# A differential, latent and stick-breaking attention trunk: another order of the latent projections, of the weight splits and of the second mixer's sums

## The chip, the cores and the metric

The kernel runs on one core of a Trainium2 chip. The metric is the device time of one execution in microseconds, a median of several runs. The engines are TensorE (PE; its weight loads are PEld in the profile), VectorE (DVE), ScalarE (ACT), GpSimd (POOL) and SyncE (SP, which here issues nearly all DMAs). Each engine runs its own list of instructions in order; they meet at semaphores.

## The reference

Two layers on one sequence of 512 frames, width 1024. Layer 0 runs two mixers on one input projection, differential attention (4 heads) and multi-head latent attention (8 heads); layer 1 runs stick-breaking attention (16 heads). Each layer ends with a SwiGLU network of inner width 2816.

```python
def diff_mla_mixer(h, pos, ...):
    a_q, a_k, a_v, b_ql, b_kvl, b_kr = split_cols(h @ w_in, AB_IN_SPLITS)  # 512,512,512,256,128,32
    ...
    q_b = (rms_norm(b_ql, b_q_a_norm) @ b_w_q_b).reshape(B, S, B_HEADS, B_NOPE_DIM + B_ROPE_DIM)
    kv_b = (rms_norm(b_kvl, b_kv_a_norm) @ b_w_kv_b).reshape(B, S, B_HEADS, B_NOPE_DIM + B_V_DIM)
    ...
    out_b = latent_attention(q_nope, q_rope, k_nope, k_rope, b_v, (B_NOPE_DIM + B_ROPE_DIM) ** -0.5)
    mixed = jnp.concatenate([out_a..., out_b...], axis=-1)
    return mixed @ w_out

def stick_breaking_attention(q, k, v, scale):      # for one block of queries lo..hi
    z = jnp.einsum('bqhd,bkhd->bhqk', q[:, lo:hi], k[:, :hi]) * scale
    sp = jnp.where(mask, jax.nn.softplus(z), 0.0)
    tail = lax.cumsum(sp, axis=3, reverse=True) - sp
    w = jnp.where(mask, jnp.exp(jax.nn.log_sigmoid(z) - tail), 0.0)
    return jnp.einsum('bhqk,bkhd->bqhd', w, v[:, :hi])

def reference(x, ...):
    for l in range(DEPTH):                          # DEPTH = 2
        h = rms_norm(x, norm_mix[l])
        x = x + (diff_mla_mixer(h, ...) if l % 2 == 0 else stick_breaking_mixer(h, ...))
        x = x + swiglu(rms_norm(x, norm_ffn[l]), ...)
    return x
```

## The kernel before, in words

**Products.** Activations lie transposed (features on partitions, 512 frames along the free axis). Each float32 product is made of three products in the fp32r format: both operands are split into a high and a low part, and high times high, high times low and low times high are summed in PSUM.

**Weights.** They come in numbered chunks `g` of 128 partitions by up to 1408 columns into three slots (`WSLOTS`) in turn. For a chunk SP issues the load into `wraw` (`load_chunk`, L312) once the low part of the chunk three earlier is made; ACT copies it into `w_hi` (`split_hi`, L319) once PE has finished the chunk three earlier; POOL subtracts, `w_lo = wraw - w_hi` (`split_lo`, L331). Where in ACT's list a split stands is written by hand (`hi_static(act, g)`); POOL takes the chunks in their order, between its other work.

**Order.** Every engine's list is written out by hand in its own block at the end of the program; the small functions (`bq_pe`, `bq_act`, `bq_dve` and so on) are called there in the order in which they run, and no planner moves them.

**Token stage.** Here the weights are the moving operand and a 128x128 tile of the activations is the stationary one, so that frames come out on the partitions. PE makes the latent projection (`lat_pe`, chunks 0 to 3), the first differential queries (`pj_pe` for p = 0, chunks 4 and 5), and then for each half `hf` of the eight latent heads four query tiles (`bq_pe`, six matmuls of 384 columns) and four key and value tiles (`bkv_pe`, three matmuls of 512 columns), chunks 6 to 9. ACT evacuates and squares a tile, DVE sums the squares (`bq_dve`; `bkv_dve` also copies the keys and makes the low part of the values). A query tile waits for the square of the tile two earlier, a key tile for DVE's low part of the tile three earlier. When all eight tiles of a half are summed, DVE makes the means (`b_mean_dve`), ACT the inverse roots (`rs_act`), POOL a Newton step (`rs_newton_pool`) and then the rotation and scaling of two heads (`b_pair_pool`, L921 to L931). Chunk 10 is split by ACT right behind `rs_act` of half 0, chunk 11 two query tiles later. `rope_kr_dve` rotates the keys that all heads share. The squares of the differential queries go through one buffer, `pj_sq`: ACT writes the second half (`qk_act`, L973) after DVE has summed the first (`qk_dve`, L995).

**Second mixer.** Eight pairs of heads. In a pair PE makes the scores of both heads (`c_scores_pe`), then projects the next pair's queries, sums the first head's tails (`c_tail_pe`, L1490), projects the keys, sums the second head's tails, multiplies with the values (`c_values_pe`, L1521) and projects the next values. Between scores and tails lie three blocks of |z|, exp and log on ACT (`c_chain_act`) and of softplus and its split on DVE (`c_chain_dve`; L1479 makes the low part, from two operands in SBUF). A tail waits for all three blocks and goes through the key blocks in order. Before the first pair's chain ACT splits three chunks in a row. In the last pair PE fills its time with products of the output projection that are already possible (`out_early_pe`, L368): output chunk 0 up to tile 5, then chunk 1, tile 6 of chunk 0, chunk 2.

**Output projection.** `out_act` waits for a finished row of x, norms it, and then splits the chunk three ahead. The three chunks of `OUT_EARLY` need only their last tile then; chunk 3 is the first that runs whole.

## Time and profile before

| | us |
|---|---|
| median of 3 runs | 1286.64 (1285.88 to 1288.28) |
| the profiled execution | 1289.69 |
| its span | 1287.9 |
| PE busy (weight loads) | 1258.3 (1071.2) |
| DVE, ACT, POOL busy | 570.0, 584.7, 528.9 |

The profile is of one execution; its durations are those of that execution, which took 3.05 us more than the median. PE's matmuls overlap, so that the distance between two starts, and not a row's own duration, tells what one costs. A row of the timeline ends with the idle time before it in brackets and with what ended it. POOL's durations are rough. PEclk is the granted clock of TensorE as a mean over a stretch, 1.00 being 2.4 GHz.

### The profile page before, as it was taken

The numbers are of one execution on the slowest core, as the hardware profiler recorded it, in microseconds if no ns is written. First come the engines' busy times: TensorE is split into PE (matmuls) and PEld (weight loads), VectorE is DVE, ScalarE is ACT, GpSimd is POOL, SyncE is SP. The second block draws the span as 40 slices with busy tenths as digits, with TensorE's granted clock in tenths as the row PEclk, the third lists the DMA queues.
The fourth block names the chain that finished last, engine by engine and source line by source line (L and its number), as shares of the span: only waits on it lengthen the run. The fifth ranks groups of instructions, "written<-read, shape, count | busy, mean of one in ns | idle before, by whom it ended". The sixth has DMA issues, their size and how long they took to land.

```text
span 1287.9 us, 16944 instructions
## 1 busy us (share of the span) xinstructions
PE 1258.3 (98%) x6308; PEld 1071.2 (83%) x6308; DVE 570.0 (44%) x995; ACT 584.7 (45%) x959; POOL 528.9 (41%) x267
## 2 busy tenths in 40 slices
PE   8899989999999999999999999998999999999999
PEld 7799978888888888888878888887888888888887
DVE  7756677653221112221278888886322210122210
ACT  5657865554322122233367777885433321222310
POOL 4465520265445344445432222221744444344442
PEclk9999999999999999999999999999999999999999
DMA  5221110033233222332211111110322242222331
GB/s 203 84 69 46 38 50 17 17 111 115 98 114 101 80 82 98 98 129 84 82 54 56 54 49 65 56 59 16 115 88 95 101 135 72 86 96 96 113 125 41
DMA packets 29143, 105.84 MB, mean 82 GB/s; under 512 B 3360, under 2 KB 3616, under 8 KB 29088
## 3 DMA queue, kind: packets, MB, share of 16 engines
q1 hardware_dynamic: 28944, 105.07, 24.5%
q8 instruction: 37, 0.61, 0.2%
q14 instruction: 18, 0.15, 0.0%
q10 hardware_dynamic: 144, 0.02, 0.0%
HBM read 102.98 MB, written 2.10 MB: 82 GB/s over the span
## 4 chain that ended last, share of the span: by engine, by line
PE 89%; DVE 7%; ACT 2%; issue 1%; POOL 1%; DMA 0%; ACTq 0%; POOLq 0%; DVEq 0%
PE bank L342 23%; PE bank L343 22%; PE bank L346 22%; PE bank L1490 4%; PE bank L1521 2%; PE bank L1117 1%; PE bank L1451 1%; PE bank L958 1%; PE bank L960 1%; PE bank L962 1%; PE bank L1066 1%; PE bank L1356 1%; PE bank L1046 1%; PE bank L1357 1%; PE bank L1358 1%
## 5 line engine op out<-in xcount | busy, mean ns | idle before, releaser
L331 POOL TENSOR_TENSOR w_lo<-wraw,w_hi 128x1024 fp32r<-128x1024 f32 (+4 forms) x180 | 456.4, 2537 | 696.7 <-ACT w_hi L319 696.7
L342 PE MATMUL bank<-h_hi,w_hi 128*128 128x512 f32 x896 | 350.8, 391 | 0.0
L343 PE MATMUL bank<-h_lo,w_hi 128*128 128x512 f32 x896 | 349.0, 389 | 0.0
L319 ACT ACTIVATE w_hi<-wraw 128x1024 fp32r<-128x1024 f32 (+4 forms) x180 | 197.9, 1101 | 236.5 <-DVE x L664 125.6
L346 PE MATMUL bank<-h_hi,w_lo 128*128 128x512 f32 x896 | 221.8, 389 | 0.0
L342 PEld LDWEIGHTS bank<-h_hi,w_hi 128*128 128x128 f32 x896 | 168.3, 188 | 35.7 <-issue 1.1
L346 PEld LDWEIGHTS bank<-h_hi,w_lo 128*128 128x128 f32 x896 | 168.2, 188 | 34.9
L343 PEld LDWEIGHTS bank<-h_lo,w_hi 128*128 128x128 f32 x896 | 168.3, 188 | 34.2
L342 PE MATMUL bank<-f_hi,w_hi 128*128 128x512 f32 x352 | 136.9, 389 | 0.0
L343 PE MATMUL bank<-f_lo,w_hi 128*128 128x512 f32 x352 | 136.9, 389 | 0.0
L627 ACT ACTIVATE f_hi<-fa 128x512 f32 (+1 forms) x44 | 27.9, 633 | 217.1 <-DVE fa L653 217.1
L650 DVE TENSOR_TENSOR fu<-bank,rstd 128x512 f32<-128x512 f32 x44 | 30.4, 691 | 194.8 <-PE bank L346 194.8
L664 DVE TENSOR_TENSOR x<-bank,x 128x512 f32<-128x512 f32 x32 | 22.1, 692 | 197.9 <-PE bank L346 197.9
L346 PE MATMUL bank<-f_hi,w_lo 128*128 128x512 f32 x352 | 85.6, 389 | 0.0
L342 PEld LDWEIGHTS bank<-f_hi,w_hi 128*128 128x128 f32 x352 | 66.1, 188 | 13.7
L346 PEld LDWEIGHTS bank<-f_hi,w_lo 128*128 128x128 f32 x352 | 66.1, 188 | 13.7
L343 PEld LDWEIGHTS bank<-f_lo,w_hi 128*128 128x128 f32 x352 | 66.1, 188 | 13.7
L648 DVE TENSOR_TENSOR fy<-bank,rstd 128x512 f32<-128x512 f32 x44 | 30.4, 692 | 101.0 <-PE bank L346 100.5
L958 PE MATMUL bank<-w_hi,h_hi 128*128 128x256 f32 x192 | 55.8, 291 | 0.0
L447 ACT ACTIVATE h_hi<-x,vec 128x512 fp32r<-128x512 f32 x32 | 23.0, 719 | 69.1 <-DVE x L664 40.2
L960 PE MATMUL bank<-w_hi,h_lo 128*128 128x256 f32 x192 | 54.3, 283 | 0.0
L962 PE MATMUL bank<-w_lo,h_hi 128*128 128x256 f32 x192 | 54.3, 283 | 0.0
(277 smaller groups left out, 2007.0 us busy)
## 6 DMA issues: line engine op xcount, KB each, us to landing
wraw<-in_w_in SPq DMA_DIRECT2D x120, 512.0 KB, 3.2
wraw<-in_w_down SPq DMA_DIRECT2D x32, 704.0 KB, 4.1
wraw<-in_w_ab SPq DMA_DIRECT2D x20, 512.0 KB, 3.3
x<-in_xt SPq DMA_DIRECT2D x8, 256.0 KB, 5.9
out<-x SPq DMA_DIRECT2D x8, 256.0 KB, 2.0
wraw<-in_w_ab SPq DMA_DIRECT2D x4, 416.0 KB, 5.9
wraw<-in_w_ab SPq DMA_DIRECT2D x2, 384.0 KB, 3.0
wraw<-in_w_ab SPq DMA_DIRECT2D x2, 256.0 KB, 2.8
```

The lines of the kernel that those rows point to most:

```text
L319: nc.scalar.activation(whi[:, s, 0:width], wraw[:, s, 0:width], ACT.Copy).then_inc(S("w_hi"), 1)
L331: nc.gpsimd.tensor_tensor(wlo[:, s, 0:width], wraw[:, s, 0:width], whi[:, s, 0:width], ALU.subtract).then_inc(S("w_lo"), 1)
L342: nc.tensor.matmul(out_bank, w, src_hi[kt], start=(kt == 0), stop=False)
L343: nc.tensor.matmul(out_bank, w, src_lo[kt], start=False, stop=False)
L346: return nc.tensor.matmul(out_bank, wlo[:, s, kt * P:(kt + 1) * P], src_hi[kt], start=False, stop=(kt == n - 1))
L627: nc.scalar.activation(tile_at(f_of[L][0], f), as3(fa[:], f), ACT.Copy).then_inc(S("net_hi"), 1)
L648: nc.vector.tensor_tensor(fy[:], bank[2 * j][:], rstd[:], ALU.mult).then_inc(S("net_y"), 1)
L650: nc.vector.tensor_tensor(fu[:], bank[2 * j + 1][:], rstd[:], ALU.mult).then_inc(S("net_u"), 1)
L958: nc.tensor.matmul(o, tok(hhi, 4 * c + k, i), whi[:, slot(g), w], start=(c == 0 and k == 0 and i % 2 == 0), stop=False, skip_group_check=True)
L960: nc.tensor.matmul(o, tok(hlo, 4 * c + k, i), whi[:, slot(g), w], start=False, stop=False, skip_group_check=True)
L962: last = nc.tensor.matmul(o, tok(hhi, 4 * c + k, i), wlo[:, slot(g), w], start=False, stop=(c == 1 and k == 3), skip_group_check=True)
L1490: last = nc.tensor.matmul(z, cmats[:, 0 if src == kb else 1, :], t[j][:, TO[src]:TO[src] + w], start=False, stop=True, skip_group_check=True)
```

## The change

Four parts:

1. **Latent queries and keys alternate** (`B_ORDER`) on PE, ACT and DVE; the last key column block (`lat_lo_dve(dve, 2)`) comes before `rope_kr_dve`, which goes behind the second query tile; `kr_trans_pe` and `kr_hi_act` go behind the half.
2. **Two square buffers**: `pj_sq` gets two halves, and the square of tile n waits for the sum of n - 2.
3. **Token-stage weights start 48 elements (192 bytes) into their slot** (`token_at`), for all chunks before `G_OB` = 20, in the load, in both splits and in the matmuls.
4. **Second mixer.** The first pair's first tail and the last pair's second tail go by source block: block `src` needs only DVE's part `src + 1`. The splits of the second and third chunk move from before the first pair's chain to behind its fourth and sixth block. Tile 6 of output chunk 0 moves from behind the last values to ahead of the last tail. `out_act` splits chunks 3 to 7 before it waits for the row of x.

```diff
+def token_at(g):
+    return 48 if g < G_OB else 0
...
-    def load_chunk(sp, g, s, src, width):
+    def load_chunk(sp, g, s, src, width, at=0):
         wait(sp, "w_lo", g - (WSLOTS - 1))
-        sp.dma_start(wraw[:, s, 0:width], src).then_inc(S(f"w_in{s}"), 16)
+        sp.dma_start(wraw[:, s, at:at + width], src).then_inc(S(f"w_in{s}"), 16)
...
     def out_act(act, g0, L, n):
         for d in range(KT):
+            if d < 5:
+                hi_static(act, g0 + d + 3)
             act.wait_ge(S("out_x"), L * KT + d + 1)
             norm_act(act, n, d)
-            hi_static(act, g0 + d + 3)
+            if d >= 5:
+                hi_static(act, g0 + d + 3)
...
+    B_ORDER = ((0, 0), (0, 1), (1, 0), (0, 2), (1, 1), (0, 3), (1, 2), (1, 3))
...
-            c = slice(k * BQ_N, (k + 1) * BQ_N)
+            c = slice(token_at(g) + k * BQ_N, token_at(g) + (k + 1) * BQ_N)
...
-        wait(act, "pj_sum", n)
-        nc.scalar.activation(pj_sq[:], bank[PJ[t]][:], ACT.Square).then_inc(S("pj_sq"), 1)
+        wait(act, "pj_sum", n - 1)
+        nc.scalar.activation(pj_sq[:, t, :], bank[PJ[t]][:], ACT.Square).then_inc(S("pj_sq"), 1)
...
     def c_tail_pe(pe, u, j):
+        if isinstance(u, int) and (u, j) in ((0, 0), (C_PAIRS - 1, 1)):
+            for src in range(NB):
+                if src < 3:
+                    pe.wait_ge(S(f"c_slo{j}"), u * 3 + (src + 1))
+                w = TW[src]
+                for kb in range(src + 1):
+                    b, o = ZAT[kb]
+                    z = bank[ZB[j][b]][:, o + TW[kb] - w:o + TW[kb]]
+                    for t in (cshi, cslo):
+                        last = nc.tensor.matmul(z, cmats[:, 0 if src == kb else 1, :], t[j][:, TO[src]:TO[src] + w],
+                                                start=False, stop=True, skip_group_check=True)
+                    if src == NB - 1 and kb != 2:
+                        last.then_inc(S(f"c_tail{j}"), 1)
+            return
         pe.wait_ge(S(f"c_slo{j}"), u * 3 + 3)
...
-            for i in range(NB):
-                bq_act(act, 0, i)
-            hi_static(act, 9)
-            for i in range(NB):
-                bkv_act(act, 0, i)
+            for what, i in B_ORDER:
+                (bq_act, bkv_act)[what](act, 0, i)
+                if (what, i) == (0, 3):
+                    hi_static(act, 9)
             kr_hi_act(act)
...
-            rope_kr_dve(dve)
             lat_lo_dve(dve, 2)
...
+            for what, i in B_ORDER:
+                (bq_dve, bkv_dve)[what](dve, 0, i)
+                if (what, i) == (0, 1):
+                    rope_kr_dve(dve)
...
                     c_chain_act(act, u, 1, 0)
+                    if late is not None:
+                        late(1)
                     c_chain_act(act, u, 1, 1)
                     c_chain_act(act, u, 1, 2)
+                    if late is not None:
+                        act.wait_ge(S("c_vy"), 1)
+                        late(2)
...
-            c_act(0, 1, lambda c: hi_static(act, G_C + 6 + c))
+            c_act(0, 1, lambda c: hi_static(act, G_C + 6 + c), lambda c: hi_static(act, G_C + 3 + c))
...
                     c_vt_pe(pe, u)
+                    if nxt is None:
+                        pe.wait_ge(S("c_mlo"), C_HEADS - 2)
+                        out_early_pe(pe, G_OUT1, 1, 0, (KT - 2,))
```

Three places show how the lists move. ACT in the token stage, before: the two squares of the first differential queries (`pj_sq`), the split of chunk 8 (`w_hi<-wraw` of 768 columns), then the query tiles (`qb` and `bq_sq`).

```order
L973 ACTIVATE pj_sq_83<-bank6 128x512
L973 ACTIVATE pj_sq_83<-bank7 128x512
L319 ACTIVATE w_hi_51<-wraw_50 128x768
L861 ACTIVATE qb_63<-bank0 128x4x96
L864 ACTIVATE bq_sq_84<-bank0 128x384
L861 ACTIVATE qb_63<-bank1 128x4x96
L864 ACTIVATE bq_sq_84<-bank1 128x384
L861 ACTIVATE qb_63<-bank0 128x4x96
L864 ACTIVATE bq_sq_84<-bank0 128x384
```

ACT at the same place now:

```order
L981 ACTIVATE pj_sq_83<-bank6 128x512
L981 ACTIVATE pj_sq_83<-bank7 128x512
L323 ACTIVATE w_hi_51<-wraw_50 128x768
L869 ACTIVATE qb_63<-bank0 128x4x96
L872 ACTIVATE bq_sq_84<-bank0 128x384
L869 ACTIVATE qb_63<-bank1 128x4x96
L872 ACTIVATE bq_sq_84<-bank1 128x384
L884 ACTIVATE vb_hi_65<-bank2 128x256
L887 ACTIVATE bk_sq_82<-bank2 128x256
L869 ACTIVATE qb_63<-bank0 128x4x96
L872 ACTIVATE bq_sq_84<-bank0 128x384
```

The key and value tiles (`vb_hi`, `bk_sq`) come in between; the rows ahead of them stand as before.

ACT at the second mixer's start, before: `cq_hi` and `ck` are the first pair's operands, `ca0` and `ca1` the chains of its two heads, three rows a block.

```order
L1543 ACTIVATE ck_119<-cyk_122 64x512 x2
L319 ACTIVATE w_hi_51<-wraw_50 128x1024 x3
L1463 ACTIVATE ca0_130<-bank0 128x512
L1465 ACTIVATE ca0_130<-ca0_130 128x512
L1467 ACTIVATE ca0_130<-ca0_130 128x512
L1463 ACTIVATE ca0_130<-bank1 128x384
```

The same place now, up to the sixth block of the chain:

```order
L1565 ACTIVATE ck_119<-cyk_122 64x512 x2
L323 ACTIVATE w_hi_51<-wraw_50 128x1024
L1471 ACTIVATE ca0_130<-bank0 128x512
L1473 ACTIVATE ca0_130<-ca0_130 128x512
```

and behind the fourth block (`ca1` from bank3):

```order
L1475 ACTIVATE ca1_131<-ca1_131 128x512
L323 ACTIVATE w_hi_51<-wraw_50 128x1024
L1471 ACTIVATE ca1_131<-bank4 128x384
L1473 ACTIVATE ca1_131<-ca1_131 128x384
L1475 ACTIVATE ca1_131<-ca1_131 128x384
L1471 ACTIVATE ca1_131<-bank5 128x512
L1473 ACTIVATE ca1_131<-ca1_131 128x512
L1475 ACTIVATE ca1_131<-ca1_131 128x512
L323 ACTIVATE w_hi_51<-wraw_50 128x1024
L1568 ACTIVATE cq_hi_117<-cyq_121 64x512 x4
```

One split is left ahead of the chain, the second stands behind its fourth block and the third behind its sixth.

PE in the last pair, before, from the transposes of the values (`cyv`) on; `cs1` is the second head's operand, `mixed` belongs to the output projection.

```order
L1566 MATMUL bank7<-mat_53,cyv_123 128x128 x4
L1490 MATMUL bank3<-cs1_hi_128,cmats_124 128x512
L1490 MATMUL bank3<-cs1_lo_129,cmats_124 128x512
L1490 MATMUL bank3<-cs1_hi_128,cmats_124 128x384
L1490 MATMUL bank3<-cs1_lo_129,cmats_124 128x384
L1490 MATMUL bank3<-cs1_hi_128,cmats_124 128x256
L1490 MATMUL bank3<-cs1_lo_129,cmats_124 128x256
L1490 MATMUL bank3<-cs1_hi_128,cmats_124 128x256
L1490 MATMUL bank3<-cs1_lo_129,cmats_124 128x256
```

The same place now:

```order
L1588 MATMUL bank7<-mat_53,cyv_123 128x128 x4
L372 MATMUL bank6<-mixed_hi_61,w_hi_51 128x512
L372 MATMUL bank6<-mixed_lo_62,w_hi_51 128x512
L372 MATMUL bank6<-mixed_hi_61,w_lo_52 128x512
L1500 MATMUL bank3<-cs1_hi_128,cmats_124 128x512
L1500 MATMUL bank3<-cs1_lo_129,cmats_124 128x512
L1500 MATMUL bank3<-cs1_hi_128,cmats_124 128x384
L1500 MATMUL bank3<-cs1_lo_129,cmats_124 128x384
L1500 MATMUL bank4<-cs1_hi_128,cmats_124 128x384
L1500 MATMUL bank4<-cs1_lo_129,cmats_124 128x384
L1500 MATMUL bank3<-cs1_hi_128,cmats_124 128x256
```

Three products of the output projection come first, and the sums take block 0 (512 columns), block 1 (384) and then block 2 (256) across the banks instead of bank after bank.

## Rows read from the trace of the kernel before

**Rows 1.** Stretches: us, busy time (instructions) of each engine, PEclk (granted clock), DMA share, GB/s
```profile
43.80:47.50 3.70, 0.14 (x1) 0.00 (x0) 2.98 (x7) 2.13 (x5) 0.73 (x1) 1.00 0.30 117
47.50:55.00 7.50, 7.32 (x29) 6.21 (x30) 4.39 (x15) 5.08 (x13) 3.95 (x3) 0.77 0.28 81
280.00:640.00 360.00, 360.00 (x1598) 298.42 (x1597) 81.13 (x117) 110.44 (x129) 171.27 (x71) 1.00 0.30 98
660.00:680.00 20.00, 17.83 (x91) 15.57 (x90) 19.52 (x28) 13.12 (x24) 4.36 (x2) 0.91 0.24 79
860.00:895.00 35.00, 31.21 (x162) 26.56 (x160) 24.22 (x42) 19.30 (x34) 2.41 (x1) 0.95 0.09 31
```

**Rows 2.** Timeline, PE, token stage: start, us, engine line op out<-in, form, [idle before <-releaser]
```profile
47.51 0.45 PE L836 MATMUL bank<-w_hi,ql_hi 128*128 128x384 f32 x1 [3.58 <-ACT bq_sq L864]
...
70.93 0.39 PE L958 MATMUL bank<-w_hi,h_hi 128*128 128x256 f32 x1
```

**Rows 3.** Timeline, ACT, token stage
```profile
45.37 0.60 ACT L973 ACTIVATE pj_sq<-bank 128x512 f32<-128x512 f32 x1 [4.00 <-DVE tiny L995]
...
58.40 1.05 ACT L319 ACTIVATE w_hi<-wraw 128x1024 fp32r<-128x1024 f32 x1
```

**Rows 4.** Timeline, DVE, token stage
```profile
40.65 0.27 DVE L790 MEMSET krpad<- 128x256 f32 x1
...
42.67 0.74 DVE L780 SCALAR_TENSOR_TENSOR kvl_lo<-bank,vec,kvl_hi 128x512 fp32r<-128x512 f32 x1
...
47.86 0.41 DVE L869 TENSOR_REDUCE tiny<-bq_sq 128x4 f32<-128x256 f32 x1
...
48.38 0.41 DVE L869 TENSOR_REDUCE tiny<-bq_sq 128x4 f32<-128x256 f32 x1
...
54.32 0.41 DVE L886 COPY kb<-bank 128x256 f32<-128x256 f32 x1
...
55.31 0.41 DVE L886 COPY kb<-bank 128x256 f32<-128x256 f32 x1
```

**Rows 5.** Timeline, POOL, token stage
```profile
59.53 2.41 POOL L331 TENSOR_TENSOR w_lo<-wraw,w_hi 128x1024 fp32r<-128x1024 f32 x1 [3.72 <-ACT w_hi L319]
...
68.49 2.39 POOL L331 TENSOR_TENSOR w_lo<-wraw,w_hi 128x1024 fp32r<-128x1024 f32 x1
```

**Rows 6.** Timeline, PE, second mixer, first pair and start of the second
```profile
665.81 0.50 PE L1490 MATMUL bank<-cs_hi,cmats 128*128 128x512 f32 x1 [2.17 <-DVE cs_lo L1479]
...
687.00 0.40 PE L1451 MATMUL bank<-cq_hi,ck 128*128 128x512 f32 x1
```

**Rows 7.** Timeline, DVE, same stretch
```profile
659.73 2.77 DVE L1479 TENSOR_TENSOR cs_lo<-cs,cs_hi 128x512 fp32r<-128x512 f32 x1
...
665.06 0.69 DVE L1479 TENSOR_TENSOR cs_lo<-cs,cs_hi 128x512 fp32r<-128x512 f32 x1
...
671.30 3.57 DVE L1558 TENSOR_TENSOR cq_lo<-cyq,cq_hi 64x512 fp32r<-64x512 f32 x2
```

**Rows 8.** Timeline, POOL, same stretch
```profile
654.62 7.34 POOL L331 TENSOR_TENSOR w_lo<-wraw,w_hi 128x1024 fp32r<-128x1024 f32 x3 [13.51 <-ACT w_hi L319]
```

**Rows 9.** Timeline, PE, second mixer, last pair and output projection
```profile
875.34 0.80 PE L1490 MATMUL bank<-cs_hi,cmats 128*128 128x512 f32 x1 [3.20 <-DVE cs_lo L1479]
...
879.58 0.39 PE L1521 MATMUL bank<-cs_hi,cv 128*128 128x512 f32 x1
...
896.31 0.50 PE L342 MATMUL bank<-mixed_hi,w_hi 128*128 128x512 f32 x1 [1.71 <-ACT w_hi L319]
```

**Rows 10.** Timeline, DVE, last pair
```profile
878.90 0.69 DVE L1509 TENSOR_TENSOR cs_lo<-bank,cs_hi 128x512 fp32r<-128x512 f32 x1
```

**Rows 11.** Timeline, PE, latent projection: tile 2 (k = 0), then tile 3 (k = 1)
```profile
11.09 0.35 PE L698 MATMUL bank<-w_hi,h_hi 128*128 128x416 f32 x1
...
13.33 0.34 PE L698 MATMUL bank<-w_hi,h_hi 128*128 128x416 f32 x1
...
14.82 0.91 PE L703 MATMUL bank<-w_lo,h_hi 128*128 128x416 f32 x4
```

More of the change, by code:

```diff
@@ L202, in trunk @@
     bk_sq, end = place("bk_sq", [P, 2, 4 * B_NOPE], F32, at=phase0 + half + half // 2)
-    pj_sq, end = place("pj_sq", [P, SEQ], F32, at=phase0 + 2 * half - 4 * SEQ)
+    pj_sq, end = place("pj_sq", [P, 2, SEQ], F32, at=phase0 + 2 * half - 2 * 4 * SEQ)
     bq_sq, end = place("bq_sq", [P, 2, 4 * B_QK], F32, at=phase0 + half // 2)
@@ L847, in bkv_pe @@
             pe.wait_ge(S("bv_lo"), n - 2)
-        o, c = bank[KV_BANK[n % 3]][:, 0:BKV_N], slice(i * P, (i + 1) * P)
-        nc.tensor.matmul(o, kvhi[:, c], whi[:, slot(g), 0:BKV_N], start=True, stop=False)
-        nc.tensor.matmul(o, kvlo[:, c], whi[:, slot(g), 0:BKV_N], start=False, stop=False)
-        nc.tensor.matmul(o, kvhi[:, c], wlo[:, slot(g), 0:BKV_N], start=False,
+        o, c, w = bank[KV_BANK[n % 3]][:, 0:BKV_N], slice(i * P, (i + 1) * P), slice(token_at(g), token_at(g) + BKV_N)
+        nc.tensor.matmul(o, kvhi[:, c], whi[:, slot(g), w], start=True, stop=False)
+        nc.tensor.matmul(o, kvlo[:, c], whi[:, slot(g), w], start=False, stop=False)
+        nc.tensor.matmul(o, kvhi[:, c], wlo[:, slot(g), w], start=False,
                          stop=True).then_inc(S("bkv" if i < NB - 1 else "chunk_done"), 1)
@@ L1589, in load_ab @@
             def load_ab(g):
-                load_chunk(sp, g, slot(g), w_ab[g, :, 0:width_of(g)], width_of(g))
+                load_chunk(sp, g, slot(g), w_ab[g, :, 0:width_of(g)], width_of(g), token_at(g))
             for d in range(KT):
@@ L1653, in lo @@
             def lo(g):
-                split_lo(pool, g, slot(g), width_of(g))
+                split_lo(pool, g, slot(g), width_of(g), token_at(g))
             def table(dst, at, gain_at, n):
@@ L1833, in _, with c_act @@
             rs_act(act, "n2", NB)
-            def c_act(u, nxt, hi):
+            def c_act(u, nxt, hi, late=None):
                 if u is not None:
@@ L1862, in c_act @@
                     c_w_act(act, u, 1, 2)
-                if nxt is not None:
+                if nxt is not None and u is not None:
                     hi(1)
@@ L1866, in c_act @@
                     cout_act(u, 0)
-                if nxt is not None:
+                if nxt is not None and u is not None:
                     act.wait_ge(S("c_vy"), nxt + 1)
@@ L2109, in _ @@
                 pj_pe(pe, 0, 1, i)
-            for i in range(NB):
-                bq_pe(pe, 0, i)
+            for what, i in B_ORDER:
+                (bq_pe, bkv_pe)[what](pe, 0, i)
             kr_trans_pe(pe)
-            for i in range(NB):
-                bkv_pe(pe, 0, i)
-            for i in range(NB):
-                bq_pe(pe, 1, i)
-            for i in range(NB):
-                bkv_pe(pe, 1, i)
+            for what, i in B_ORDER:
+                (bq_pe, bkv_pe)[what](pe, 1, i)
             for i in range(NB):
```

49 lines of the change are left out of this document (19 added, 30 removed).

## The prediction, as it was written before the kernel ran

> **What bounds the kernel now.** I read the stretches first. From 280 to 640 us PE is busy for 360.00 of 360 us at full clock, and it stays so in most of the rest; nothing that the change does there can count [rows 1]. Time is to be had where PE waits. The reader should see three such places. From 43.8 to 47.5 us PE does 0.14 us of work, and in the 7.5 us behind it the granted clock is 0.77, so that (1 - 0.77) x 7.5 = 1.7 us more are lost. From 660 to 680 and from 860 to 895 PE is busy for 17.83 of 20 and 31.21 of 35 us, at a clock of 0.91 and 0.95: by the same sum 1.8 us each [rows 1]. In all three the clock fell behind a wait, from 2.4 GHz to its lower level of 1.2 GHz for a while.
>
> Then I read the timeline of each engine at these places, since a wait has its cause two or three engines away. In the token stage PE waits 3.58 us for ACT's first square of a query tile [rows 2]. ACT itself had waited 4.00 us before the second square of the differential queries, until DVE had summed the first half out of the only buffer [rows 3], and DVE was late since the rotation of the shared keys stood ahead from 40.65 on and the last low part came only at 42.67 [rows 4]. From there the wait is handed on: ACT splits chunk 10 at 58.40 [rows 3], POOL makes its low part at 59.53 and, behind the Newton step and the first pair of heads, that of chunk 11 at 68.49 [rows 5], and PE begins with chunk 11 at 70.93, 2.44 us after that start, the moment that POOL is done [rows 2]. So the row that sets the time of all that follows is the one at 70.93, and POOL, started by ACT's split, sets it.
>
> The last number of the second mixer's first pair is the first score of the second, 687.00 [rows 6]. In the last pair it is the first matmul of output chunk 3, 896.31 [rows 9].
>
> **Token stage: queries and keys alternate, two buffers.** The second square no longer waits for the sum. PE has its bank full at about 41.8, so ACT squares at 41.9 instead of 45.37, splits chunk 8 and has the first query tile out at about 44. PE then alternates: a query tile's wait (the square of the tile two earlier) lies beside a key tile. At 32 columns more than the width, which is the pace of rows 11 (416 columns in 0.187 us), the 48 matmuls of 384 columns and 24 of 512 take 8.3 + 5.4 us, with the transposes some 14.3: from 41.68 to about 56. The 3.58 us go, and so should the low clock behind them.
>
> What is late next is DVE. It is at 40.65 when the two low parts are made. From 42.67 to ACT's second square at 45.37 it made the third low part, about 0.65, and one set of the differential queries, so 1.95 [rows 3, 4]; the third part and two sets bring it to 45.2 now. A query tile costs 48.38 - 47.86 = 0.52 us, a key tile 55.31 - 54.32 = 0.99 [rows 4]. Four of each are 6.0; the rotation took 2.0 before (42.67 - 40.65), partly behind POOL's low part of chunk 7, and I estimate 0.85 for it with POOL idle, and 0.3 for the means. That gives 52.4 for the means of half 0, then some 0.6 on ACT for the roots: the split of chunk 10 starts at 53.1 instead of 58.40, 5.3 earlier. POOL follows with the same distances: 54.2 for the low part of chunk 10, 8.96 later (68.49 - 59.53 [rows 5]) that of chunk 11, 2.4 for itself: PE begins chunk 11 at 65.6 instead of 70.93. Term: **-5.3**. PE does not bind: it ends its tiles at 56.3, starts chunk 10 at 56.7, is through at 62.4, waits 0.8 for POOL's first pair and, after the head transposes, 1.4 for chunk 11. Those are new waits of 2.2 us, and if the clock falls behind them 1.7 come back. Bounds: -3.0 (the clock falls and DVE's rotation runs into a POOL instruction as before) to -5.9.
>
> **192 bytes.** No instruction is added, the load moves as many bytes. Before, tile 2 of the latent projection reads its weights from the slot's start and takes 2.24 us for 12 matmuls (0.187 each); tile 3 reads from 1664 bytes in, and 8 matmuls take 1.49 us (0.186) [rows 11]. So 128-byte steps do nothing; 192 is a multiple of 64 only, which no row shows. I take 0. Bounds: the 576 + 84 + 72 = 732 matmuls of the stage each cost 32 columns at 2.4 GHz (13 ns) beyond their width; gone altogether that would be -9.8, doubled +9.8. I stay at the row, since two offsets cost the same.
>
> **Second mixer, first pair.** ACT's two splits in front of the chain go: 2 x 0.97, of which 1.1 reach the first block, since its scores come that much before the chain began. POOL is then idle while DVE makes its low parts. Before, one of these took 2.77 us at 659.73 against 0.69 at 665.06 [rows 7], and it ended 0.5 us after POOL's three low parts, which ran from 654.62 to 661.96 [rows 8]. So the first head's blocks are ready at about 662.3 instead of 665.7 (3.2 earlier and more: 1.1 + 2.1), and PE, which ends the queries at 663.6, goes on without the wait of 2.17 [rows 6]. That saves 2.3 and the low clock behind. The order by source block adds nothing here, since all blocks are there by then.
>
> But the low parts of the weights now stand in the second head's blocks. ACT splits at 662.1, 666.3 and, for the next chunk, 669.7, so that POOL runs from 663.2 to 665.6, 667.4 to 669.8 and 670.9 to 673.3, and DVE starts its three low parts at 663.4, 667.6 and 671.3: each inside one. At about 2 us each that is 6 us against the two blocked instructions of before (2.1, and 2.2 in the pair that took 3.57 from 671.30 on [rows 7]), and DVE reaches the first head's weights at 675.1, as late as before (674.87). PE, early by 4, waits for it: 1.9 ahead of the second tail, then 0.5, 0.6 and 1.0 in the values. It begins the second pair at 686.8 against 687.00. The Trainium skill, "SBUF — State Buffer", who interferes with whom, gives the rule: VectorE and GpSimd share a port pair "and it's an exclusive lock", for a VectorE instruction with two SBUF inputs. The two long rows agree with it, and it speaks against this edit; without it, the whole 3.9 would stay.
>
> The margin is thin: the first of the three starts 0.2 after POOL's, and would it come first, 2 us are saved. I take **-0.5**, between 0.2 and 2 and nearer to the blocked end. Bounds: -3.9 (none is blocked) to +1.5 (all three, and the low clock comes while PE projects the values).
>
> **Last pair.** Tile 6 of output chunk 0 and the tails of source blocks 0 and 1 run in the 3.20 us that PE waited for DVE's third block [rows 9]. When this comes, at about 875.3, 14 matmuls of 256 columns are left, 1.7 us: PE is through at 877.0 and not at 879.58 [rows 9]. The values don't gain that much. They need DVE's low part of the first head's third block, which starts at 878.90 [rows 10] and is not moved: the last four matmuls start at 879.6 and end at 880.05, against 880.85 (879.58 and the eight matmuls of rows 9's second row, 1.27): -0.8. Tile 6 no longer stands behind the values: three matmuls of 0.227, -0.7. And ACT splits output chunk 3 as soon as chunk 0 is done, at about 891.6, so that its high part is there at 892.8 when PE asks at 892.9: the wait of 1.71 [rows 9] goes with 0.15 for the refill of PE's pipeline. Term: **-3.4**. ACT's later splits stand before waits that the split's own condition meets already; the norms behind them come one split (1 us) later, with five whole chunks, 27 us, of cover. Bounds: -1.6 (only the wait at the end, the low clock falling into output chunk 1) to -4.0.
>
> **The sum.** -5.3 - 0.5 - 3.4 = -9.2. The new waits lie in the same three places and are of the size behind which the clock fell before (2.2, 3.9 in parts, 1.6 in one piece). I count one low stretch of 1.7 us among them, which gives -7.5: the profiled execution, 1289.69 with a span of 1287.9, would come to 1282.2 (span 1280.4). The runs' median is 3.05 lower, 1286.64, and I take the same difference from it: **1279.1**.
>
> **Rivals.**
>
> *The lock doesn't bite.* DVE's low parts miss POOL's: for it, that DVE instructions between them read PSUM and shift by tenths; against it, the three computed overlaps. 3.4 more: 1275.7. Chance 0.13.
>
> *The clock eats it.* A low stretch behind each of the three new waits: for it, that it fell behind all three old ones; against, that the new are cut in pieces. 3.4 less: 1282.5. Chance 0.18.
>
> *DVE hides the token stage's gain.* POOL's low parts of chunks 8 and 9 and its addition meet DVE's rotation and its means, and the halves end only 2 us earlier instead of 5.3: 1282.4. Chance 0.08.
>
> *The offset costs, on the slower side.* At 192 bytes each moving read takes some columns more. It decides the sign from 7.5 / 732 = 10 ns a matmul on, some 25 columns at 2.4 GHz; with the doubled 32 columns the 576 matmuls of 256 columns, which PE does without a pause, cost 7.7, the rest 2.1 of which half is hidden: 1288. For it: nothing shows such an offset; against: the two offsets of rows 11. Chance 0.04. The other sign, 1270: 0.02.
>
> *It does nothing*: the waits move to the next engine and come back. Against it stands that PE is saturated behind each place, so that what it gains there stays: 1286, chance 0.05.
>
> **How the numbers follow.** The forecast has 0.50. From 1275.7 to 1282.5 lie forecast and three rivals; the clock can fall once more or once less elsewhere, too (1.7 us either way). Range **1274.8 to 1283.6**, which leaves out some 0.15. About 0.2% (2.6 us) is what a measurement of this kernel can tell from no change. Faster than 1284.1: 0.50 + 0.13 + 0.17 + 0.07 + 0.02 and a bit of the rest, 0.90. Within: 0.06. Slower: 0.04.
>
> **What would show it.** Right: no wait over 1 us on PE from 42 to 56; ACT's second square at once behind the first; POOL's low part of chunk 11 starting near 63 and PE behind it near 65.6, with waits of 0.8 and 1.4 ahead. In the first pair no wait ahead of the first tail but one near 1.9 ahead of the second, and DVE rows of 2.5 us under POOL's. In the last pair the values still ending with DVE's third low part, and no wait for the split of output chunk 3. Wrong: matmuls of 256 columns at another distance than 0.12 us (the offset counts); the distance from ACT's split of chunk 10 to PE's chunk 11 other than 12.5 us; the second pair starting over 2 us early (no lock); or a granted clock under 1 in none or all of the three places.

## The result, and the profile after

| | kernel before | changed kernel |
|---|---|---|
| median, us (runs) | 1287.36 (4) | 1279.15 (4; 1277.01 to 1279.58) |
| profiled execution, us; its span | 1289.69; 1287.9 | 1279.58; 1277.8 |
| stretches of lower clock ahead of the last 5 us | 3.41 + 6.83 + 3.41 + 3.41 us | 6.83 us |

The ratio is 0.9929 [0.9912, 0.9947]; a second set of runs on another chip gave 0.9914 [0.9894, 0.9934] (1279.01 beside 1290.43). The change makes the kernel faster: in the first set by 8.2 us between the two medians and 9.1 us by the ratio; the span of the profiled execution is 10.1 us shorter.

The stretches of the changed kernel, with the columns of [rows 1]:

```profile
43.80:47.50 3.70, 3.70 (x21) 3.44 (x20) 3.67 (x14) 3.11 (x9) 1.45 (x1) 1.00 0.66 225
56.00:66.00 10.00, 8.00 (x60) 7.08 (x61) 5.88 (x20) 5.77 (x14) 9.44 (x14) 1.00 0.16 54
280.00:640.00 360.00, 360.00 (x1599) 298.34 (x1598) 82.57 (x121) 109.90 (x129) 166.75 (x67) 1.00 0.30 98
660.00:680.00 20.00, 17.19 (x84) 13.52 (x83) 19.53 (x27) 10.89 (x19) 7.41 (x3) 1.00 0.22 75
853.50:886.20 32.70, 30.47 (x160) 24.72 (x158) 23.30 (x40) 19.36 (x34) 2.42 (x2) 1.00 0.11 34
```

Where PE did 0.14 us of work in 3.7 it now does 3.70; the middle of the kernel is as full as before; the clock is 1.00 in all three places, where it had been 0.77, 0.91 and 0.95 [rows 1]. Between 660 and 680 PE works less than before (17.19 of 20 us): that is the first pair, below.

Token stage, PE: the start of chunk 10, the wait ahead of the first transposes of the heads, and the start of chunk 11, which answers to 70.93 in [rows 2]:

```profile
56.97 0.38 PE L966 MATMUL bank<-w_hi,h_hi 128*128 128x256 f32 x1
...
63.61 0.29 PE L1149 MATMUL bank<-mat,qb 128*96 128x128 f32 x1 [0.72 <-issue]
...
65.86 0.39 PE L966 MATMUL bank<-w_hi,h_hi 128*128 128x256 f32 x1 [1.20 <-POOL w_lo L335]
```

ACT's second square, which waits no longer for DVE, and its split of chunk 10 [rows 3]:

```profile
41.98 0.60 ACT L981 ACTIVATE pj_sq<-bank 128x512 f32<-128x512 f32 x1 [0.39 <-PE bank L970]
...
53.38 1.04 ACT L323 ACTIVATE w_hi<-wraw 128x1024 fp32r<-128x1024 f32 x1
```

POOL's low parts of chunks 10 and 11 [rows 5], 8.97 us apart where 8.96 was expected:

```profile
54.50 2.42 POOL L335 TENSOR_TENSOR w_lo<-wraw,w_hi 128x1024 fp32r<-128x1024 f32 x1 [1.82 <-ACT w_hi L323]
...
63.47 2.34 POOL L335 TENSOR_TENSOR w_lo<-wraw,w_hi 128x1024 fp32r<-128x1024 f32 x1
```

From ACT's split of chunk 10 to PE's chunk 11 it is 12.48 us (12.53 before). Chunk 11 starts 5.07 us earlier.

Second mixer, first pair. DVE's low parts of the second head's blocks, all three long now [rows 7]:

```profile
656.19 2.78 DVE L1487 TENSOR_TENSOR cs_lo<-cs,cs_hi 128x512 fp32r<-128x512 f32 x1
...
660.46 2.65 DVE L1487 TENSOR_TENSOR cs_lo<-cs,cs_hi 128x384 fp32r<-128x384 f32 x1
...
664.20 2.75 DVE L1487 TENSOR_TENSOR cs_lo<-cs,cs_hi 128x512 fp32r<-128x512 f32 x1
```

and POOL's low parts beside them [rows 8]:

```profile
656.00 2.42 POOL L335 TENSOR_TENSOR w_lo<-wraw,w_hi 128x1024 fp32r<-128x1024 f32 x1 [6.30 <-ACT w_hi L323]
...
660.25 2.44 POOL L335 TENSOR_TENSOR w_lo<-wraw,w_hi 128x1024 fp32r<-128x1024 f32 x1 [1.83 <-ACT w_hi L323]
...
663.83 2.57 POOL L335 TENSOR_TENSOR w_lo<-wraw,w_hi 128x1024 fp32r<-128x1024 f32 x1 [1.14 <-ACT w_hi L323]
```

Each DVE row starts 0.2 to 0.4 us behind a POOL row and ends 0.4 to 0.6 us behind its end. On PE [rows 6] the first tail waits for nothing, the second for DVE, and so do two value tiles; the second pair's first score is the fifth row:

```profile
647.06 0.47 PE L1459 MATMUL bank<-cq_hi,ck 128*128 128x512 f32 x1 [0.85 <-DVE ck L1576]
...
667.00 0.50 PE L1512 MATMUL bank<-cs_hi,cmats 128*128 128x512 f32 x1 [1.65 <-DVE cs_lo L1487]
...
671.29 0.44 PE L1543 MATMUL bank<-cs_hi,cv 128*128 128x384 f32 x1 [0.32 <-DVE cs_lo L1531]
...
672.61 0.38 PE L1543 MATMUL bank<-cs_hi,cv 128*128 128x256 f32 x1 [0.71 <-DVE cs_lo L1531]
...
680.06 0.40 PE L1459 MATMUL bank<-cq_hi,ck 128*128 128x512 f32 x1
```

From the first pair's first score to the second's it is 33.00 us, against 32.61 before (654.39 to 687.00). This part has lost 0.39 us.

Last pair and output projection, PE [rows 9]: the third block is waited for 0.85 us instead of 3.20, and output chunk 3 starts without a wait:

```profile
868.36 0.39 PE L1500 MATMUL bank<-cs_hi,cmats 128*128 128x256 f32 x1 [0.85 <-DVE cs_lo L1487]
...
872.66 0.38 PE L1543 MATMUL bank<-cs_hi,cv 128*128 128x256 f32 x1 [0.70 <-DVE cs_lo L1531]
...
886.16 0.50 PE L346 MATMUL bank<-mixed_hi,w_hi 128*128 128x512 f32 x1
```

From the last pair's first score (860.61 before, 853.63 now) to output chunk 3: 32.53 us instead of 35.70, so -3.17.

In the span the 10.1 us are: -5.07 to chunk 11, -2.26 from there to the first pair's first score (where the forecast had nothing), +0.39, -0.04 over pairs 2 to 7, -3.17.

### The profile page after: what moved, and what is told of

Read it like the earlier page. It is cut to its first block, busy times and chain, and to the rows that moved or that the text cites. A ratio compares the mean times of both kernels' runs of the same rounds, so it can differ in the third digit from the quotient of the medians.

```text
span 1277.8 us, 16943 instructions
## 1 busy us (share of the span) xinstructions
PE 1253.7 (98%) x6308; PEld 1064.7 (83%) x6308; DVE 569.3 (45%) x995; ACT 583.9 (46%) x959; POOL 528.7 (41%) x267
## 4 chain that ended last, share of the span: by engine, by line
PE 88%; DVE 8%; ACT 1%; issue 1%; POOL 1%; DMA 0%; POOLq 0%
PE bank L346 23%; PE bank L347 22%; PE bank L350 22%; PE bank L1512 3%; PE bank L1543 2%; PE bank L1459 1%; PE bank L1125 1%; PE bank L966 1%; PE bank L970 1%; PE bank L968 1%; PE bank L1074 1%; PE bank L1364 1%; PE bank L1365 1%; PE bank L1054 1%; PE bank L372 1%
```

## The experiments

In the later sets of runs the kernel before has medians of 1290.0 to 1290.4, about 3 us more than in the first; whether the chip or chance made that isn't shown. So the later medians are compared with 1279.0, the changed kernel in such a set (`after_again`). They mix in the low clock, which comes and goes from one execution to the next (see "The low clock"), so that differences of 1 to 3 us between medians are rough, and the traces decide. "Heads" is the time from the first transpose of the eight-head loop to the first of the differential heads behind it.

| kernel | median, us | ratio [95%] | chunk 11 starts | heads, us |
|---|---|---|---|---|
| before | 1290.0 | | 70.93 | 85.16 |
| changed | 1279.01 | 0.9914 [0.9894, 0.9934] | 65.86 | 83.12 |
| no_offset | 1281.64 | 0.9936 [0.9922, 0.9949] | 65.89 | 84.49 |
| offset_only | 1288.99 | 0.9995 [0.9986, 1.0004] | 71.09 | 84.23 |
| dist64 | 1280.87 | 0.9938 [0.9918, 0.9958] | 65.87 | 84.12 |
| one_square | 1281.76 | 0.9940 [0.9918, 0.9962] | 67.25 | 84.21 |
| undo_two | 1280.70 | 0.9927 [0.9903, 0.9951] | | |
| placed | 1275.88 | 0.9882 [0.9867, 0.9898] | 65.76 | 83.12 |
| early10 | 1274.26 | 0.9880 [0.9861, 0.9899] | 64.43 | 83.12 |
| cs448 | 1272.12 | 0.9860 [0.9838, 0.9882] | 64.19 | 83.16 |

### Does the offset count?

```diff
 def token_at(g):
-    return 48 if g < G_OB else 0
+    return 0
```

> The changed kernel with the weights of the token stage back at the slot's start, all else as changed. Theory A (the offset counts): the matmuls of 256 columns stand 0.120 us apart again, the stretch of the eight heads takes 85.1 us instead of 83.1, and the time is 2.3 us (0.29 from the start of chunk 11 to the first head, 1.97 in the heads) over the changed kernel's 1279.2: 1281.4. Rival (the forecast's value, nothing for the offset; the 2.3 come from other things of the token stage being earlier): 1279.2, and the heads at 83.1 us.

> The changed kernel once more, beside the other kernels of this study on one chip. By its first runs 0.9929 of the kernel before, 9.1 us less. Both theories of the offset expect the same; the run gives the distance to the others: 1.7 us under the kernel without the offset if what the two traces show at the heads is all, nothing if the forecast's value stands.

The heads take 84.49 us, the stretch from chunk 11 to the first head 8.26 us against 7.97, and the median is 2.6 us over the changed kernel's (1281.64 and 1279.01, in sets on two chips, with intervals of the ratios that overlap): by the traces 1.66 us belong to the offset (0.29 + 1.37). Theory A stands in that the offset counts, but 85.1 was too much. The kernel without the offset keeps 0.67 of the 2.04 us that the heads gained, so something else is in them (`one_square`, below).

The kernel before with the offset and nothing else:

> The kernel before with the weights of the token stage 192 bytes into their slots, nothing else changed. Theory A: 2.3 us less than the kernel before, 1285.1 where that has 1287.4, with 0.1133 us between 256-column matmuls from the first chunk of queries on; the wait of 3.58 us and all four stretches of lower clock stay. Rival: no change, 1287.4.

It gives 0.9995 [0.9986, 1.0004]: no change that can be told, as the rival has it, and not theory A's 2.3 us. By the trace the heads are 0.93 us shorter. The matmuls have the quick pace here too, and most heads take 11.79 to 11.81 us instead of 12.04. But the two that took 12.37 us before still do: there PE waits for ACT's exponentials, and what it gains it waits longer (why, `one_square` shows). So the offset is worth 0.93 us in the heads with one square buffer and 1.37 with two.

To measure the disputed cost by itself, a program of matmuls alone in groups of 24, whose operands lie at chosen offsets (one execution):

> Not the kernel: matmuls alone, in groups of 24 with as many columns, as many bytes of offset of the moving and of the stationary operand (within 512) as a table says, nothing beside them; the output is not computed. Theory A (the 192 bytes of the weights, the moving operand, speed up matmuls of 256 columns): distance of two starts 0.120 us with the moving operand at 128 bytes as in the kernel before, 0.1133 us at 320 as in the changed kernel, with the stationary operand at 384 in both; 384 and 416 columns at 0.173 and 0.187 at either offset, as in the traces of both kernels. Theory B (it is not the offset but what runs beside it in the changed kernel): 0.120 at every offset. Theory C (it is the distance of the moving operand from the stationary one): the 0.1133 moves with the stationary operand's offset.

Its rows on PE: the last three of the group with the moving operand at 128 bytes and the start of the next, then the last three of that one, with it at 320, and again the start of the next:

```profile
34.10 0.28 PE L199 MATMUL bank<-w_hi,h_hi 128*128 128x256 f32 x1
34.22 0.28 PE L199 MATMUL bank<-w_hi,h_lo 128*128 128x256 f32 x1
34.34 0.28 PE L199 MATMUL bank<-w_lo,h_hi 128*128 128x256 f32 x1
34.46 0.29 PE L199 MATMUL bank<-w_hi,h_hi 128*128 128x256 f32 x1
...
36.86 0.28 PE L199 MATMUL bank<-w_hi,h_hi 128*128 128x256 f32 x1
36.98 0.28 PE L199 MATMUL bank<-w_hi,h_lo 128*128 128x256 f32 x1
37.09 0.28 PE L199 MATMUL bank<-w_lo,h_hi 128*128 128x256 f32 x1
37.20 0.28 PE L199 MATMUL bank<-w_hi,h_hi 128*128 128x256 f32 x1
```

Three matmuls take 0.36 us in the one and 0.34 in the other. Over the steady part of each group, from the starts:

| stationary minus moving, bytes modulo 512 | 256 columns, us each |
|---|---|
| 0 or 256 | 0.1200 (5 groups) |
| 128 or 384 | 0.1188 (6) |
| 192 or 448 | 0.1178 (6) |
| 64 or 320 | 0.1133 (2), 0.1178 (3) |

So it is the distance of the two operands (theory C), not the offset of the one. Three more groups, with another place in the PSUM bank or at the end of the program, repeat the paces of their distances, 0.1200 and 0.1133; distances of 288 and 352, tried once each, gave about 0.118 and 0.117. In the kernel before the distance was 256, the worst; 192 bytes more make it 64. At 64 or 320 there are two steady paces for the same distance, and the changed kernel shows both: chunks 4, 5, 11 and most of the heads' at 0.1133 to 0.1140, chunks 10 and 12 at 0.1178. In `after_again`, the same kernel once more, chunks 10 and 12 have the quick pace and chunk 11 the slow one. So it isn't the addresses that choose; what does stays open. The distance that helps 256 columns hurts 512: 0.2267 at 0 and 256, 0.2333 at 64. For 384 and 416 columns the four offsets tried differ by 0.003 and 0.0016 us, so the latent projection [rows 11] could show nothing.

> The changed kernel with the weights 64 bytes instead of 192 into their slots, all else as changed. By the sweep it is the distance from the moving to the stationary operand that counts, in bytes modulo 512: 256 and 0 gave 0.120 us for 256 columns, 128 and 384 gave 0.1188, odd multiples of 64 gave 0.1178 or 0.1133. At 64 bytes the distance is 192, an odd multiple as with 192 bytes (64). Theory C (any odd multiple of 64 does): chunks at 0.1178 and 0.1133 again, the eight heads in 83.1 to 83.7 us, the time within 1 us of the changed kernel's. Rival (64 alone, or the 192 bytes as such): all chunks at 0.1178 or 0.120, the heads in 84.0 to 84.5 us as in the kernel without the offset, 0.9 to 1.7 us over the changed kernel.

All groups of the stage stand at 0.1176 to 0.1179 and none at 0.1133, and the heads take 84.12 us. Theory C as I had widened it (any odd multiple of 64) falls: the quick pace comes at 64 or 320 alone, in the sweep as here.

### What the second buffer does

```diff
-        wait(act, "pj_sum", n - 1)
-        nc.scalar.activation(pj_sq[:, t, :], bank[PJ[t]][:], ...
+        wait(act, "pj_sum", n)
+        nc.scalar.activation(pj_sq[:, 0, :], bank[PJ[t]][:], ...
```

> The changed kernel with one buffer for the squares again, the order of tiles as changed. Theory S (the second buffer takes the wait, the order keeps DVE's rotation out of its way): ACT's second square waits for DVE's first sum again, to about 44.5 us, the first query tile is out 2.5 us later than in the changed kernel, DVE catches up a part, and PE begins chunk 11 at 66.9 to 67.4 instead of 65.86: 1.0 to 1.6 us over the changed kernel. Rival O (the order alone did it, since DVE sums as soon as the low parts are made): chunk 11 at 65.9 to 66.2.

Chunk 11 starts at 67.25, 1.39 us later, as theory S has it, though ACT's second square came at 43.79 and not 44.5. So with one buffer the new order alone has 3.68 of the 5.07 us up to chunk 11, and the second buffer the rest; two buffers in the old order were not run. But the median is 2.75 us up: the heads take 84.21 us, 1.09 more, with the periods of 12.37 us back (12.38 and 12.36). The kernel before shows why, on ACT in the heads:

```profile
102.25 0.60 ACT L973 ACTIVATE pj_sq<-bank 128x512 f32<-128x512 f32 x1 [2.17 <-DVE tiny L995]
102.88 0.59 ACT L1125 ACTIVATE mixed_hi<-bank 64x512 fp32r<-64x512 f32 x1
103.50 0.48 ACT L1083 ACTIVATE pn<-bank,tiny 128x256 f32<-128x256 f32 x1
```

With one buffer ACT waits 2.17 us for DVE's sum in the heads too, and the exponentials behind it come too late for PE. Where the matmuls have the quick pace this shows as a wait, here in `one_square`:

```profile
104.81 0.33 PE L1054 MATMUL bank<-mat,pn 128*128 128x128 f32 x1 [0.21 <-ACT pn L1103]
```

That is the 0.67 us at the old pace; at the quick pace the same buffer is worth 1.09.

### Who took the first pair's gain?

ACT's splits of the third late chunk and of the next pair's queries are moved to where ACT waited 3 us:

```diff
                     c_chain_act(act, u, 1, 2)
-                    if late is not None:
-                        act.wait_ge(S("c_vy"), 1)
-                        late(2)
...
-                    hi(0)
+                    if late is None:
+                        hi(0)
...
                     for b in range(1, 3):
                         c_w_act(act, u, 0, b)
+                    if late is not None:
+                        late(2)
+                        hi(0)
```

> The changed kernel, with the splits of the third late chunk and of the next pair's query chunk on ACT behind the first head's weights of the first pair, where ACT waited 3 us, instead of inside and behind the second head's chain. Theory L (DVE's low parts are held up for as long as POOL makes one, and this is what took the first pair's gain): of the three DVE rows of 2.7 us only the first stays, the second and third take 0.56 and 0.69; PE waits neither ahead of the second tail (1.65) nor in the values (1.03 and the refills, 2.0 in all): the second pair starts 3.0 to 3.8 us earlier after the first pair's first score, 29.2 to 30.0 us instead of 33.0, and the time is 1275.4 to 1276.2. Rival P (the first pair is bound by ACT's and DVE's own work, and POOL only fills gaps): at most 1 us less, 1278.2 or more.

DVE's low parts of the second head's blocks and one of the weights:

```profile
656.08 2.77 DVE L1487 TENSOR_TENSOR cs_lo<-cs,cs_hi 128x512 fp32r<-128x512 f32 x1
...
660.35 0.56 DVE L1487 TENSOR_TENSOR cs_lo<-cs,cs_hi 128x384 fp32r<-128x384 f32 x1
...
662.00 0.69 DVE L1487 TENSOR_TENSOR cs_lo<-cs,cs_hi 128x512 fp32r<-128x512 f32 x1
...
666.42 0.56 DVE L1531 TENSOR_TENSOR cs_lo<-bank,cs_hi 128x384 fp32r<-128x384 f32 x1
```

POOL, for the same time:

```profile
655.88 2.42 POOL L335 TENSOR_TENSOR w_lo<-wraw,w_hi 128x1024 fp32r<-128x1024 f32 x1 [6.29 <-ACT w_hi L323]
...
665.22 2.41 POOL L335 TENSOR_TENSOR w_lo<-wraw,w_hi 128x1024 fp32r<-128x1024 f32 x1 [6.91 <-ACT w_hi L323]
```

and PE's second tail, without a wait, and the second pair's first score:

```profile
646.95 0.47 PE L1459 MATMUL bank<-cq_hi,ck 128*128 128x512 f32 x1 [0.85 <-DVE ck L1576]
...
665.12 0.39 PE L1512 MATMUL bank<-cs_hi,cmats 128*128 128x512 f32 x1
...
675.98 0.40 PE L1459 MATMUL bank<-cq_hi,ck 128*128 128x512 f32 x1
```

Only the low part that still lies beside POOL's is long (2.77); the others take 0.56 and 0.69. The pair takes 29.03 us instead of 33.00, 3.97 less, and the median is 3.1 us under the changed kernel's. Theory L is shown: it was the position of POOL's work, not the amount. That ACT's list got lighter at this place is not the cause, since the second low part begins 13.40 us behind the pair's first score in both kernels (660.46 - 647.06, 660.35 - 646.95) and only its own length differs, 2.65 and 0.56. And the row at 666.42 lies inside POOL's from 665.22 on and takes 0.56 us: it reads one operand from PSUM, and isn't held. In the changed kernel 20 such instructions (L1531) lie beside one of POOL's, and all take 0.56 or 0.69 us, as without it. The Trainium skill, "SBUF — State Buffer", who interferes with whom, has the lock for an instruction of VectorE with two SBUF inputs; these rows agree with it.

### The low clock

Matmuls alone again, in one execution, with pauses between stretches of 25 us:

> Not the kernel: matmuls of 512 columns alone, in stretches of 110 (25 us) with a pause between two stretches, made by copies on ACT: 14 pauses from about 0.5 to 4.3 us, three of them in two pieces with 8 matmuls between; the output is not computed. Theory K (the lower clock comes behind a pause when that is long enough, and the changed kernel's waits are below that length): full clock behind the pauses up to that of 1.65 us that the changed kernel has, half behind all from some length on, at the latest that of 3.58 us of the kernel before. Rival (it is luck of the moment, or comes from what the other engines do): no order by length, or no lower clock at all in this program.

The waits that PE shows for three of the pauses, and the 7.5 us behind each:

```profile
147.74 0.50 PE L202 MATMUL bank<-w_hi,h_hi 128*128 128x512 f32 x1 [1.67 <-ACT pad L190]
...
174.84 0.50 PE L202 MATMUL bank<-w_hi,h_hi 128*128 128x512 f32 x1 [1.88 <-ACT pad L190]
...
231.62 0.50 PE L202 MATMUL bank<-w_hi,h_hi 128*128 128x512 f32 x1 [2.61 <-ACT pad L190]
```
```profile
147.80:155.30 7.50, 7.50 (x33) 6.22 (x34) 0.00 (x0) 0.00 (x0) 1.00 0.00 0
174.90:182.40 7.50, 7.50 (x26) 6.03 (x27) 0.00 (x0) 0.00 (x0) 0.77 0.00 0
231.70:239.20 7.50, 7.50 (x33) 6.18 (x34) 0.00 (x0) 0.00 (x0) 1.00 0.00 0
```

The clock is 1.00 behind the pause of 1.67 us and behind all shorter ones, nine in all, the three in two pieces among them (the largest 1.67 + 0.72). Of the five longer ones, the clock fell behind 1.88, 3.04 and 3.98 us and not behind 2.09 and 2.61. Theory K holds in its first half as far as nine pauses go: no fall behind waits such as the changed kernel's 1.65 and 1.20 us. In its second half it does not: from 1.88 us on the clock may fall or not.

The kernels agree. Both have one more wait near 180 us, behind the last differential head, that the change leaves alone, before and after:

```profile
187.91 0.33 PE L1046 MATMUL bank<-mat,pn 128*128 128x128 f32 x1 [1.92 <-DVE pn L1239]
```
```profile
180.49 0.33 PE L1054 MATMUL bank<-mat,pn 128*128 128x128 f32 x1 [1.90 <-DVE pn L1247]
```

Right behind these transposes PE waits again, 1.30 and 1.41 us. Here each has its stretch of 6.83 us at 1.2 GHz, from 188.76 and 181.45 on; in `no_offset`, `dist64`, `one_square`, `undo_two` and `cs448` it is 3.41 us at the same place. Of the changed kernel's first four executions one (1277.01) has a mean granted clock of 1.000, so the clock stayed up there too. So the same kernel has this stretch in one execution and not in another, and it is worth up to 3.4 us. In the traces of all kernels here the clock fell, between 24 us and the last 5, only behind waits of 1.88 us or more, and never behind one of 1.72 or less by itself.

### Two parts undone

```diff
-            if d < 5:
-                hi_static(act, g0 + d + 3)
             act.wait_ge(S("out_x"), L * KT + d + 1)
             norm_act(act, n, d)
-            if d >= 5:
-                hi_static(act, g0 + d + 3)
+            hi_static(act, g0 + d + 3)
...
-        if isinstance(u, int) and (u, j) in ((0, 0), (C_PAIRS - 1, 1)):
+        if isinstance(u, int) and (u, j) in ((C_PAIRS - 1, 1),):
```

> The changed kernel with two of its parts undone, in places 200 us apart, so that the trace tells them apart: ACT splits output chunks 3 to 7 behind the norms again, and the first pair's first tail is written by output block again. By the forecast's steps: the wait for the split of output chunk 3 comes back, 1.7 us with 0.15 for the refill, so that this chunk starts 1.4 to 1.9 us later; the first pair's order adds nothing (0.0 to 0.1), since all its source blocks are there by then. Rival for the first: the wait has gone because all else in the last pair is earlier, and it does not come back (under 0.5). Rival for the second: the tail waits for the third block, held by POOL's low part, 1 us or more, and the second pair starts later by that.

```profile
887.29 0.50 PE L346 MATMUL bank<-mixed_hi,w_hi 128*128 128x512 f32 x1 [1.72 <-ACT w_hi L323]
```

The wait is back with 1.72 us, and from the last pair's first score (852.89) to output chunk 3 it is 34.40 us, 1.87 more, as the forecast's step had it (1.71 + 0.15). The first pair takes 33.00 us as in the changed kernel, and its order by source block does nothing there.

### Towards a better kernel

PE's wait of 1.20 us ahead of chunk 11 ends with POOL, which starts with ACT's split of chunk 10. Beside `placed`:

```diff
             for what, i in B_ORDER:
                 (bq_act, bkv_act)[what](act, 1, i)
+                if (what, i) == (0, 0):
+                    hi_static(act, 10)
                 if (what, i) == (0, 1):
                     rs_act(act, "b0", 48)
-                    hi_static(act, 10)
```

> The kernel of the run placed, with ACT's split of chunk 10 one query tile earlier, ahead of the second tile of half 1 instead of behind it and the roots of half 0. Theory (POOL, started by this split, sets the start of chunk 11): the split at 52.0 instead of 53.4, POOL's low part of chunk 10 at 53.1, of chunk 11 at 62.1, PE begins chunk 11 at 64.5 instead of 65.8, 1.3 us less than placed: 1274.6 where placed has 1275.9. Rival (POOL's low part then meets DVE's means at 52.64 and holds them, or DVE waits for the later tile): the means at 55, nothing gained, or 0.5 us lost.

```profile
53.03 2.40 POOL L335 TENSOR_TENSOR w_lo<-wraw,w_hi 128x1024 fp32r<-128x1024 f32 x1 [0.34 <-ACT w_hi L323]
...
62.01 2.37 POOL L335 TENSOR_TENSOR w_lo<-wraw,w_hi 128x1024 fp32r<-128x1024 f32 x1
```
```profile
64.43 0.39 PE L966 MATMUL bank<-w_hi,h_hi 128*128 128x256 f32 x1 [0.88 <-POOL w_lo L335]
```

The low parts start at 53.03 and 62.01, chunk 11 at 64.43, 1.33 us earlier than in `placed`, and the median is 1.6 us lower.

Last, the distance of 64 in the second mixer:

```diff
+    end += 448
     (cz0, cz0lo), end = pair("cs0", [P, TWS], at=end)
```

> The kernel of the run early10 with the second mixer's log and weight tiles (moving operand of its tails and values) 448 bytes further, so that the distance to the stationary operand (the sums' matrices, the values) is 64 bytes modulo 512 instead of 0. Theory C, refined (at 64 modulo 256, 256 columns take 0.1133 or 0.1178 us, 512 columns 0.233 instead of 0.227): some 260 matmuls of 256 columns gain 2.2 to 6.7 ns each, 0.6 to 1.7 us, and 60 of 512 lose 6.7 ns, 0.4 us: 0.2 to 1.3 us less than early10, with steps of 0.113 to 0.118 us in the tails. Rival (in groups that change their width and their stationary operand from one matmul to the next the distance does nothing, or the loss of the 512 columns prevails): 0.120 in the tails, and the time as early10 or up to 0.5 us more.

In a steady pair the 256-column matmuls of the tails stand 0.115 us apart instead of 0.120, as the refined theory has it, and those of 512 columns 0.2334 instead of 0.2266. But from the first pair's first score to the last pair's it is 202.63 us, and 202.62 in `early10`. In the pair looked at, each of the two tails takes 2.77 us instead of 2.83, so the narrow ones win there; the values behind them take 1.62 instead of 1.49, most of it in one step of 0.30 instead of 0.18. The time is as the rival has it, the reason that it gives is not; what holds the values isn't shown. The median is 2.1 us lower, with ranges that overlap (1271.01 to 1273.45 against 1271.67 to 1275.27). Of the 0.7 us between the two spans the second mixer has none, and the trace has one stretch of lower clock of 3.41 us near 180 us where `early10` has 6.83. So I don't put the 2.1 down to the edit. Both kernels are faster than the changed kernel; which of them is the better is open.

## Why the prediction was right, and where it was not

The time came out at 1279.15 where 1279.1 was forecast. The two large steps, in the token stage and in the last pair, came out within 0.3 us, and that carried it into the range. That it agrees to 0.1 us is luck, since two errors of 2.6 us cancel. The change is worth 10.1 us in the profiled executions and not 7.5. And the distance of 3.05 us from profiled execution to median, which I carried over, is 0.4 for the changed kernel: the kernel before, of which three runs were shown (median 1286.64), has 1290.0 as the median of 35 runs in all sets, so that its profiled execution was an ordinary one and the three were quick ones.

Step by step:

- **Token stage, -5.3 to chunk 11: right** in mechanism and size: -5.07. The split of chunk 10 was expected at 53.1 and came at 53.38, POOL's low part of chunk 11 at 63.2 and 63.47, PE's start at 65.6 and 65.86, with waits of 0.72 and 1.20 where 0.8 and 1.4 were expected.
- **Missed: the second buffer in the heads.** I followed the buffer to the first use only. ACT squares two more such pairs beside the heads, waited for the sum there too (2.17 us at 102.25), and held up PE: -0.67 by `no_offset`, and `one_square` brings the long periods back.
- **192 bytes, taken at 0: wrong.** The step that failed is "So 128-byte steps do nothing; 192 is a multiple of 64 only, which no row shows. I take 0." The rows showed 416 columns, which hardly react to any offset; the 576 matmuls have 256. What counts is the distance of the two operands. It is worth 1.66 us (`no_offset`), inside the bounds of 9.8, on the side to which I gave 0.02. I had rows for one width and took them for another.
- **First pair, -0.5: mechanism right, size and sign off.** All three overlaps of POOL and DVE came: POOL's low parts were computed from 663.2, 667.4 and 670.9 on and began at 656.00, 660.25 and 663.83, which is 663.3, 667.6 and 671.2 in the count of the kernel before (7.33 us later), and the wait ahead of the second tail was 1.65 (1.9 forecast). The mis-sized term is the saving: PE comes to the second tail 3.47 us earlier counted from the first score and not 3.9 (21.76 us before, 18.29 without the wait of 1.65). From the second tail's start to the end of the values it takes 6.21 us instead of 4.11, 2.10 more, where 0.5, 0.6 and 1.0 were forecast. The rest of the miss is that -0.5 gave some weight to a low part that would slip past POOL, and none did. Measured +0.39. That the order by source block does nothing here was right (`undo_two`), and that the lock took the gain too: with one held instruction instead of three, `placed` needs 29.03 us, 3.6 less than before.
- **Last pair, -3.4: right**: -3.17. The wait for the third block is 0.85, the values end with DVE's low parts, and the wait for the split of output chunk 3 is gone, worth 1.87 (`undo_two`).
- **The low clock, +1.7: wrong.** The step was "The new waits lie in the same three places and are of the size behind which the clock fell before". Their sums are (0.72 + 1.20, then 1.65 with 0.32 and 0.71 in the values), but not the single waits: these reach 1.65 and 1.20 us, the old ones were 2.17, 3.20 and 3.58, and the pauses put the lowest fall at 1.88. The pieces were added up, and in the pauses no pair of pieces, up to 1.67 + 0.72, brought a fall. The clock stayed at 1.00 in all three places.

The deviations are +0.2, -0.7, -1.7, +0.9, +0.2 and -1.7, together -2.8, where the span came out 2.6 under the forecast's; the rest is rounding and stretches that differ by 0.1 or less.

## What to carry to other kernels

When a buffer or a wait is changed in a helper, follow every caller of it: the second use in the loop was worth 0.67 us that nobody had looked for. When VectorE instructions with two SBUF operands are on the critical path, place GpSimd's long ones where VectorE reads PSUM: moving two splits gave 3.97 us, where the reordering around them had lost 0.39. Before an address is called neutral, measure it with the width in question: rows of 416 columns said nothing of 256. And judge a forecast of a few us on a span, not on a median of three runs.

## What the runs showed of the hardware that I had not expected

- The pace of fp32r matmuls of 256 columns depends on the distance, modulo 512 bytes, between moving and stationary operand: 0.1200, 0.1188, 0.1178 or 0.1133 us (table above). At 64 and 320 it has two steady values, and in the same kernel a chunk had one value in one execution and the other in the next.
- 512 columns go the other way: 0.2267 us at 0 and 256, 0.2333 at 64.
- Behind pauses of up to 1.67 us the lower clock never came (nine pauses); behind five from 1.88 to 3.98 us it came three times, for 3.41 us each, and not in order of their length. In the kernels' traces it came behind waits of 1.88 us and more, and not behind 1.72 and less.
